# Sums of squares added on VectorE, the recurrent layer's heads token-major, and a small root that loads ScalarE's table early

## The chip, the cores and the metric

The kernel runs on one core of one Trainium2 chip. The metric is the device time of one launch in microseconds (us); the number given is the median of several launches. Everything is float32. TensorE does the matrix products, VectorE and ScalarE the elementwise work, and transfers are started from the queues of SyncE and GpSimd.

## The reference

The program is a chain of two transformer stacks over 256 tokens of width 1024. The first stack has two layers, each with a mixer (attention variants), a cross-attention to a memory and a gated feed-forward part. The second stack has four layers, each with a mixer (gMLP in layers 0 and 3, latent attention in layer 1, a gated recurrence in layer 2) and a convolutional feed-forward part. Every part starts with an RMS norm of the residual stream x, and the last norm makes the output:

```python
def rmsnorm(x, g):
    y = x * lax.rsqrt(jnp.mean(x * x, axis=-1, keepdims=True) + EPS)
    return y * g
```

The recurrent mixer ends so (o has 8 heads of 128 values per token; g is the last quarter of the projection h @ w_in):

```python
    o = rmsnorm(o, norm_g).reshape(B, S, nv) * jax.nn.silu(g)
    return o @ w_o
```

## The kernel before

x and h lie in SBUF as 8 tiles of 128 features by 256 tokens (features on the partitions). All weights come in one stream through a ring of 11 slabs of 8 tiles, which SyncE's queue refills as TensorE releases them. A linear of kind "F" makes one 128x256 output block after the other (8 blocks for the ones that end in x), with K matmuls each: K is 8 for `ab_out`, `nsa_out`, `mla_o`, `hg_o`, 4 for `memo0/1`, 16 for `gm_out0/3` and 22 for `down0/1` and `cdown0..3`. The blocks alternate between PSUM banks 0 and 1; VectorE (`residual`, L1054) adds block n into x[:, n], and ScalarE (`squares`, L801) then writes its square into h[:, n]. The order on every engine is written out by hand; engines meet at semaphores.

The norm: `with_norm` (L509) is called by `linear` after each block. `norm_part(k)` multiplies a 128x128 matrix of ones with the square tile h[:, k], so that the sum over features lands on all partitions of bank 4; it does so for k = n-2 after block n, and for k = 6 and 7 as well after the last block. Then ScalarE takes the root (L818), VectorE the reciprocal (L1042) and eight scaled products into h (L1045), in the second stack ScalarE adds a shift to each (L825), and TensorE's next linear takes each h tile as it comes. There are 16 norms: `mix0` and `mem` at the start have no linear ahead of them, the other 14 go through `with_norm`. After `mem0` and `mem1` TensorE first has `memk`, which reads the memory and not h.

In the down linears VectorE also reduces tiles of the modulation weights between the blocks (`ada_tile`, L1214; up to three per block), whose transfers GpSimd's queue starts.

The recurrent layer (layer 2; from L712 for TensorE, L988 for ScalarE, L1581 for VectorE): decayed scores are built in nine levels. For one level VectorE makes the arguments (L1624, L1625), ScalarE takes Exp (L1010), VectorE multiplies (L1637, L1639), TensorE multiplies (`level`) and VectorE places the result under masks (L1656). `level` runs between the blocks of `hg_v` and `hg_g`; ScalarE applies Silu to the gate blocks as they come (L1006), so that Exp and Silu alternate. After level 8, TensorE makes the 8 head outputs features-major (banks 7 and 3), VectorE copies them out (L1680), ScalarE squares (L1013), TensorE sums with ones, ScalarE takes 8 roots (L1016), VectorE takes for each head a reciprocal of 128x256 (L1684) and two products (L1685, L1687), and `hg_o` starts on head k as it is ready.

Of the kernel before, what the change touches and what calls it, by code (L numbers as in the profile page):

```python
# [8 lines left out]
ALU = mybir.AluOpType  # L9
# [139 lines left out]
def build(nc, stream, adaw_d, crow_d, xin, memin, cols_d, rows_d, gmrows_d, gmws_d, cmpw_d, consts_d, pos_d, out_d):  # L149
    with ExitStack() as ctx:  # L150
# [17 lines left out]
        stat = sb("stat", [P, 7, 56])  # L168
        att_s = sb("att_s", [P, 3, 3, 2])

        pair01 = ctx.enter_context(nc.psum_tensor("pair01", [P, 2, 512], F32))
# [74 lines left out]
        HGB = (5, 6, 7, 4)  # L246
        hg_lb = view(2048 * 8 + 3584, 8, DK)


# [120 lines left out]
        for i in range(LAYERS2):  # L370
            for n in ("mix", "ffn"):
                SHIFTED[f"{n}2_{i}"] = len(SHIFTED)

        SOURCE = {"mem0": "ab_out", "ffn0": "memo0", "mix1": "down0", "mem1": "nsa_out", "ffn1": "memo1",
# [64 lines left out]
        def _(pe):  # L439
# [173 lines left out]
            def body():  # L613
# [63 lines left out]
                for i in range(LAYERS2):  # L677
# [34 lines left out]
                    else:  # L712
# [24 lines left out]
                        n = hg_first[9]  # L737

                        pe.wait_ge(sem("hg_read"), n)
                        for hd in range(HG_HEADS):  # L740
                            if hd >= 2:
                                pe.wait_ge(sem("hg_o_read"), hd - 1)
                            ob = banks[TB[hd % 2]]
                            v = [hg_v[:, t, hd * P:hd * P + P] for t in range(TT)]
                            mm(ob[:, 0:P], v[0], hg_a[:, 0, hd, :], True, True)
                            mm(ob[:, P:TOK], v[0], hg_a[:, 2, hd, :], True, False)
                            mm(ob[:, P:TOK], v[1], hg_a[:, 1, hd, :], False, True).then_inc(sem("hg_o"), 1)
                        for hd in range(HG_HEADS):
                            pe.wait_ge(sem("hg_sq"), hd + 1)
                            if hd >= 2:  # L750
                                pe.wait_ge(sem("hg_sum_read"), hd - 1)
                            mm(banks[SB[hd % 2]][:, 0:TOK], ones, hg_e[:, hd, :], True, True).then_inc(sem("hg_sum"), 1)
                        linear("hg_o", lambda k: hg_q[:, k, :],
# [38 lines left out]
        def _(act):  # L792
# [122 lines left out]
            def body():  # L915
# [44 lines left out]
                for i in range(LAYERS2):  # L960
# [27 lines left out]
                    else:  # L988
# [12 lines left out]
                        lin = PLAN["hg_g"]  # L1001
                        for lv in range(8):
                            if lv >= 4:
                                for t in (2 * lv - 8, 2 * lv - 7):
                                    act.wait_ge(sem("mm_done"), lin.g0 + t + 1)
                                    nc.scalar.activation(hg_g[:, t, :], banks[(lin.g0 + t) % 2][:, 0:TOK],  # L1006
                                                         ACT.Silu).then_inc(sem("freed_act"), 1)
# [3 lines left out]
                        for hd in range(HG_HEADS):  # L1011
                            act.wait_ge(sem("hg_o_read"), hd + 1)
                            nc.scalar.activation(hg_e[:, hd, :], hg_b[:, hd, :], ACT.Square).then_inc(sem("hg_sq"), 1)  # L1013
                        for hd in range(HG_HEADS):
                            act.wait_ge(sem("hg_sum"), hd + 1)
                            nc.scalar.activation(hg_Q[:, hd, :], banks[SB[hd % 2]][:, 0:TOK], ACT.Sqrt, bias=EPS_COL,  # L1016
                                                 scale=1.0 / P).then_inc(sem("hg_sum_read"), 1)
                    squares(f"ffn2_{i}", x, h)
# [8 lines left out]
        def _(dve):  # L1027
# [25 lines left out]

            def residual(name, gate=None, between=None):  # L1054

                lin = PLAN[name]
                for n in range(DK):
                    g = lin.g0 + n
# [174 lines left out]
            def memory(i):  # L1233
# [30 lines left out]
                attention(*(U_MEM0, U_MEM1)[i])  # L1264
                residual(f"memo{i}")

            def body():
# [128 lines left out]
                attention(*U_DSA)  # L1396
                residual("ab_out")
                normalise("mem0", x, col("norm_mem0", 0, DK))
# [3 lines left out]
                up_tiles(0)  # L1402
                residual("down0", None, ada_tiles((2, 2, 2, 2, 2, 2, 1, 0)))
                V.engine_nop().then_inc(sem("hid_free"), 1)
# [84 lines left out]
                for kind in range(3):  # L1489
                    attention(*U_NSA[kind])  # L1490
                residual("nsa_out")
                normalise("mem1", x, col("norm_mem1", 0, DK))
# [10 lines left out]

                residual("down1", None, down1_between)
                for i in range(LAYERS2):
# [3 lines left out]
                    if i % 3 == 0:  # L1509
# [26 lines left out]
                        for f in range(GM_INNER // P):  # L1536
# [8 lines left out]
                            V.tensor_tensor(u, u, t2, ALU.mult).then_inc(sem("gm_mixed"), 1)  # L1545
                        residual(f"gm_out{i}", gate)
                    elif i % 3 == 1:
# [31 lines left out]
                        attention(*U_MLA)  # L1579
                        residual("mla_o", gate)  # L1580
                    else:  # L1581
# [95 lines left out]
                        placed(8)  # L1677
                        for hd in range(HG_HEADS):
                            dve.wait_ge(sem("hg_o"), hd + 1)
                            V.tensor_copy(hg_b[:, hd, :], banks[TB[hd % 2]][:, 0:TOK]).then_inc(sem("hg_o_read"), 1)  # L1680
                        for hd in range(HG_HEADS):
                            dve.wait_ge(sem("hg_sum_read"), hd + 1)
                            dve.wait_ge(sem("freed_act"), FREER[PLAN["hg_g"].g0 + hd][1])
                            link(V.reciprocal(hg_K[:, hd, :], hg_Q[:, hd, :]))  # L1684
                            link(V.scalar_tensor_tensor(hg_b[:, hd, :], hg_b[:, hd, :], col("hg_norm"), hg_K[:, hd, :],  # L1685
                                                        ALU.mult, ALU.mult))
                            V.tensor_tensor(hg_q[:, hd, :], hg_b[:, hd, :], hg_g[:, hd, :], ALU.mult  # L1687
                                            ).then_inc(sem("hg_y"), 1)
                        residual("hg_o", gate)
                    gate, gain = fin[:, 1, 0:DK], fin[:, 1, DK:2 * DK]  # L1690
# [11 lines left out]

                    residual(f"cdown{i}", gate, down_between)
                normalise("final", x, col("final", 0, DK), signal="out_ready")
# [131 lines left out]
```

## Time and profile before

| | us |
|---|---|
| median of 3 launches | 2768.84 (2767.59 to 2771.78) |
| the profiled execution's own time | 2776.93 |
| its span in the profile | 2775.1 |
| TensorE matmuls busy | 2612.3 (94% of the span) |
| VectorE busy | 1082.3 (39%) |
| ScalarE busy | 480.5 (17%) |
| TensorE's mean granted clock | 0.947 of 2.4 GHz |

The span is that of one profiled execution; the times are of launches without the profiler. One float32 matmul appears as two records of TensorE. Busy time of an engine overlaps with that of others; what sets the end is read in the chain of waits, which goes back from the last instruction to what released each step.

### The profile page before, as it was taken

What the parts mean: (1) busy time and instruction counts of PE and PEld (TensorE: products, weight loads), DVE (VectorE), ACT (ScalarE), POOL (GpSimd) and SP (SyncE); (2) the same over time, 40 slices, a digit from 0 to 9 for tenths busy, and PEclk for the clock granted to TensorE, in tenths of its full rate; (3) what the DMA queues carried; (4) which work ended last, traced back from release to release, by engine and by line L of the source; (5) the groups of instructions that cost most, each with busy time, mean ns of one, the idle gap of its engine ahead of it and who ended that gap; (6) DMA issues with size and microseconds to landing.
All of it is one profiled execution on the core that took longest, in us unless ns stands there. A gap on an engine that the chain in (4) does not pass through costs nothing.

```text
span 2775.1 us, 30582 instructions
## 1 busy us (share of the span) xinstructions
PE 2612.3 (94%) x11580; PEld 2052.4 (74%) x11580; DVE 1082.3 (39%) x2184; ACT 480.5 (17%) x1132; POOL 109.6 (4%) x211
## 2 busy tenths in 40 slices
PE   8789999998898999999999899999979999999997
PEld 4365888655567888588888478888768886688886
DVE  2744122245732022242563435633754552332321
ACT  1122100014402000111210222102322201102210
POOL 0000000000000000000011001110000010000000
PEclk9779999995699999999999999999989999999999
DMA  6123467530034566434778137783316774433441
GB/s 233 47 83 142 136 198 234 198 122 3 6 127 159 174 225 223 150 123 146 257 252 293 61 121 250 251 301 131 114 52 239 256 269 170 170 123 130 152 153 52
DMA packets 122174, 452.83 MB, mean 163 GB/s; under 512 B 13760, under 2 KB 13888, under 8 KB 121408
## 3 DMA queue, kind: packets, MB, share of 16 engines
q1 hardware_dynamic: 92880, 338.24, 35.2%
q0 software_dynamic: 29168, 112.80, 12.0%
q8 instruction: 93, 1.52, 0.2%
q14 instruction: 33, 0.27, 0.0%
HBM read 449.93 MB, written 1.05 MB: 163 GB/s over the span
## 4 chain that ended last, share of the span: by engine, by line
PE 88%; DVE 6%; issue 3%; ACT 2%; DMA 0%; SPq 0%; DVEq 0%; ACTq 0%; POOL 0%
PE pair L443 83%; PE bank L443 5%; DVE att_s L1136 1%; DVE arena L1131 1%; ACT arena L842 1%; PE bank L539 1%; DVE arena L1684 1%; ACT arena L854 0%; PE bank L566 0%; DVE arena L1545 0%; DVE arena L1541 0%; DMA cst<-consts_dram 0%; ACT arena L833 0%; DVE arena L1389 0%; DVE arena L1146 0%
## 5 line engine op out<-in xcount | busy, mean ns | idle before, releaser
L443 PE MATMUL pair<-h,ring 128*128 128x256 f32 x5120 | 1119.0, 382 | 26.3 <-issue 26.3
L443 PEld LDWEIGHTS pair<-h,ring 128*128 128x128 f32 x5120 | 979.9, 192 | 164.8 <-issue 29.8
L443 PE MATMUL pair<-arena,ring 128*128 128x256 f32 x3312 | 740.7, 383 | 12.6 <-DVE arena L1687 9.6
L443 PEld LDWEIGHTS pair<-arena,ring 128*128 128x128 f32 x3312 | 633.2, 192 | 106.5 <-DVE arena L1687 13.7
L443 PE MATMUL pair<-ring,h 128*128 128x512 f32 (+1 forms) x768 | 333.7, 596 | 20.9 <-issue 18.0
L443 PEld LDWEIGHTS pair<-ring,h 128*128 128x128 f32 x768 | 147.3, 196 | 202.9 <-issue 194.8
L1214 DVE CUSTOM_DVE_ANT_0 adat<-adat,crow,cols 128x1024 f32<-128x1024 f32 x192 | 241.8, 1277 | 4.2 <-DMA adat<-adaw_dram 4.2
L813 ACT ACTIVATE h<-x 128x256 f32<-128x256 f32 x120 | 49.2, 416 | 903.2 <-DVE x L1064 508.4
L1192 DVE SCALAR_TENSOR_TENSOR arena<-pair,cols,arena 128x255 f32<-128x255 f32 x176 | 84.9, 483 | 292.6 <-ACT arena L890 292.6
L890 ACT ACTIVATE arena<-pair,cols 128x256 f32<-128x256 f32 x176 | 99.2, 563 | 475.3 <-PE pair L443 475.3
L1064 DVE SCALAR_TENSOR_TENSOR x<-pair,fin,x 128x256 f32<-128x256 f32 x64 | 31.0, 484 | 378.2 <-PE pair L443 378.2
L443 PE MATMUL pair<-arena 128*128 128x128 f32 (+7 forms) x922 | 144.9, 368 | 20.6 <-DVE arena L1374 8.6
L401 POOL DMA_DIRECT2D adat<-adaw_dram x192 | 101.3, 528 | 1360.0 <-DVE mod L1214 1334.7
L443 PEld LDWEIGHTS pair<-arena 128*128 128x128 f32 (+4 forms) x922 | 99.2, 226 | 59.6 <-issue 20.6
L1077 DVE COPY arena<-pair 128x512 f32<-128x512 f32 (+1 forms) x58 | 39.1, 676 | 264.1 <-PE pair L443 264.1
L1180 DVE TENSOR_TENSOR arena<-pair,arena 128x256 f32<-128x256 f32 x44 | 18.7, 424 | 255.3 <-PE pair L443 255.3
L443 PE MATMUL bank<-arena 128*128 128x128 f32 (+2 forms) x640 | 89.1, 355 | 11.3 <-ACT arena L854 6.4
L1062 DVE TENSOR_TENSOR x<-pair,x 128x256 f32<-128x256 f32 x48 | 20.4, 424 | 201.7 <-PE pair L443 201.7
L443 PEld LDWEIGHTS bank<-arena 128*128 128x128 f32 (+2 forms) x640 | 62.8, 196 | 36.7 <-ACT arena L854 17.5
L1194 DVE SCALAR_TENSOR_TENSOR arena<-pair,cols,arena 128x254 f32<-128x254 f32 x176 | 84.7, 481 | 6.3
L842 ACT ACTIVATE arena<-arena,att_s 128x256 f32<-128x256 f32 (+2 forms) x160 | 67.6, 423 | 100.8 <-DVE att_s L1136 100.0
L443 PE MATMUL bank<-h,cst 128*128 128x256 f32 x240 | 71.1, 393 | 13.0 <-DMA cst<-consts_dram 10.8
(187 smaller groups left out, 1218.5 us busy)
## 6 DMA issues: line engine op xcount, KB each, us to landing
ring<-stream_dram SPq DMA_DIRECT2D x638, 512.0 KB, 3.9
adat<-adaw_dram POOLq DMA_DIRECT2D x192, 512.0 KB, 4.5
arena<-gmrows_dram POOLq DMA_DIRECT2D x2, 2560.0 KB, 10.1
arena<-cmpw_dram POOLq DMA_DIRECT2D x1, 2112.0 KB, 8.2
x<-x_in_dram SPq DMA_DIRECT2D x2, 512.0 KB, 4.6
arena<-mem_in_dram SPq DMA_DIRECT2D x1, 1024.0 KB, 12.5
arena<-gmws_dram POOLq DMA_DIRECT2D x2, 512.0 KB, 12.1
out_dram<-h POOLq DMA_DIRECT2D x1, 1024.0 KB, 4.1
```

The costliest lines, as they stand in the source:

```text
L401: pool.dma_start(adat[:, n % ADA_RING, :], adaw_d[n]).then_inc(sem(f"ada_in{n % ADA_RING}"), 16)
L443: return nc.tensor.matmul(out, lhsT, rhs, start=start, stop=stop)
L539: last = nc.tensor.transpose(banks[TB[j % 2]][:, b * P:b * P + P], src, ident)
L813: nc.scalar.activation(dst[:, k, :], src[:, k, :], ACT.Square).then_inc(sem("sq_done"), 1)
L842: ins = nc.scalar.activation(p, p, ACT.Exp, bias=att_s[:, u % 3, 0, e:e + 1], accum_out=att_s[:, u % 3, 1, e:e + 1])
L890: nc.scalar.activation(ybuf[:, t % 4, :], banks[g % 2][:, 0:TOK], ACT.Identity, bias=col(f"conv_b{i}", t), scale=col(f"conv_w{i}", 2 * 2 * ...
L1064: ins = V.scalar_tensor_tensor(x[:, n, :], b, gate[:, n:n + 1], x[:, n, :], ALU.mult, ALU.add)
L1077: V.tensor_copy(dst(n % 2, n // 2 * 512, w), banks[g % 2][:, 0:w]).then_inc(sem("freed_dve"), 1)
L1131: ins = V.scalar_tensor_tensor(p, s, un["scale"], un["mask"].unsqueeze(1).broadcast_to([P, 2, nk]), ALU.mult, ALU.add)
L1192: link(V.scalar_tensor_tensor(y[:, 1:TOK], b[:, 0:TOK - 1], col(f"conv_w{i}", 2 * FT + t), y[:, 1:TOK], ALU.mult, ALU.add))
L1194: V.scalar_tensor_tensor(y[:, 2:TOK], b[:, 0:TOK - 2], col(f"conv_w{i}", t), y[:, 2:TOK], ALU.mult, ALU.add).then_inc(sem("freed_dve"), 1)
L1214: V.tensor_tensor_reduce(out=w, in0=w, in1=crow[:, :], scale=1.0, scalar=col(f"ada_b{i}", t), op0=ALU.mult, op1=ALU.add, accum_out=mod[:, ...
```

## The change

Every `residual` also adds square tiles in place on VectorE: after block n it adds h[:, n-1] into h[:, 0]. TensorE then sums only h[:, 0] and h[:, 7], both after the last block. ScalarE takes a root of one column behind the sixth square. In the recurrent layer a gate block is only copied out and Silu is applied to four blocks at once; levels 3 to 6 follow gate blocks 0 to 3; the heads are made token-major ahead of gate blocks 4 to 7; their sums, roots and reciprocals are 128x8; the heads are turned back by TensorE's transposes. The diff, cut to its core:

```diff
+            def norm_sum(name):
+                pe.wait_ge(sem("sq_added"), SQ_ADDED[name])
+                mm(banks[SUMB][:, 0:TOK], ones, h[:, 0, :], True, False)
+                pe.wait_ge(sem("sq_done"), DK * (NORMS[name] + 1))
+                mm(banks[SUMB][:, 0:TOK], ones, h[:, DK - 1, :], False, True).then_inc(sem("sum_done"), 1)
-            def with_norm(norm, lag=2):
+            def with_norm(norm):
                 def after(n):
-                    if n >= lag:
-                        norm_part(norm, n - lag)
                     if n == DK - 1:
-                        for k in range(DK - lag, DK):
-                            norm_part(norm, k)
+                        norm_sum(norm)
...
# squares, ScalarE
                     nc.scalar.activation(dst[:, k, :], src[:, k, :], ACT.Square).then_inc(sem("sq_done"), 1)
+                    if lin is not None and k == DK - 3:
+                        nc.scalar.activation(spare[:, :], EPS_COL, ACT.Sqrt)
...
# residual, VectorE
+                def add_squares(k):
+                    dve.wait_ge(sem("sq_done"), DK * NORMS[norm] + k + 1)
+                    if k > 1:
+                        dve.wait_ge(sem("sq_added"), SQ_ADDED[norm] - (DK - 2) + k - 1)
+                    V.tensor_tensor(h[:, 0, :], h[:, 0, :], h[:, k, :], ALU.add).then_inc(sem("sq_added"), 1)
...
                     ins.then_inc(sem("freed_dve"), 1)
+                    if n >= 2:
+                        add_squares(n - 1)
                     if between is not None:
                         between(n)
...
# recurrent layer, TensorE (heads_out: per half, 4 matmuls for token tile 0 and 8 for tile 1, into banks 3, 2 / 5, 6;
# heads_turned: per half, two jobs of 4 transposes into banks 7 and 4, behind hg_scaled and hg_y)
-                        linear("hg_g", hin, None, lambda g: g % 2 == 1 and level(3 + g // 2))
-                        level(7)
-                        level(8)
+                        def after_gate(g):
+                            if g < 4:
+                                level(3 + g)
+                            if g == 3:
+                                level(7)
+                                level(8)
+                                pe.wait_ge(sem("hg_read"), hg_first[9])
+                                heads_out(0)
+                                heads_out(1)
+                            if g == 6:
+                                heads_turned(0)
+                            if g == 7:
+                                heads_turned(1)
+                        linear("hg_g", hin, None, after_gate)
...
# recurrent layer, ScalarE (gate_out: copy of a gate block; gates_silu: Silu of 128x1024)
                             if lv >= 4:
-                                for t in (2 * lv - 8, 2 * lv - 7):
-                                    ... Silu of gate block t
+                                gate_out(lv - 4)
...
+                        gates_silu(0)
+                        for q4 in range(2):
+                            for t in range(TT):
+                                act.wait_ge(sem("hg_o_read"), 2 * q4 + t + 1)
+                                nc.scalar.activation(hg_o2[:, t, 512 * q4:512 * q4 + 512],
+                                                     hg_o[:, t, 512 * q4:512 * q4 + 512], ACT.Square
+                                                     ).then_inc(sem("hg_sq"), 1)
+                            act.wait_ge(sem("hg_sums"), q4 + 1)
+                            r = stat[:, 1, 8 * q4:8 * q4 + 8]
+                            nc.scalar.activation(r, r, ACT.Sqrt, bias=EPS_COL, scale=1.0 / P).then_inc(sem("hg_root"), 1)
+                            gate_out(4 + 2 * q4)
+                            gate_out(5 + 2 * q4)
+                        gates_silu(4)
...
# recurrent layer, VectorE (heads_read: two copies of 128x512; heads_sums: two reductions of 128x512 to 4;
# heads_scale: reciprocal of 128x8, two products of 128x512; heads_gated: four products of 128x256 out of PSUM,
# turned head x norm gain x gate)
+                        heads_read(0)
+                        heads_sums(0)
+                        heads_read(1)
+                        heads_scale(0)
+                        heads_sums(1)
+                        heads_scale(1)
+                        heads_gated(0)
+                        heads_gated(1)
```

## Rows read from the trace of the kernel before

**Rows 1.** The page: the chain that ended last, shares by engine.
```profile
PE 88%; DVE 6%; issue 3%; ACT 2%; DMA 0%; SPq 0%; DVEq 0%; ACTq 0%; POOL 0%
```
**Rows 2.** Groups by form, whole span: count | busy us, mean ns | idle before, releasers.
```profile
L443 PE MATMUL bank<-h,cst 128*128 128x256 f32 x240 | 71.1, 393 | 13.0 <-DMA cst<-consts_dram 10.8 <-ACT h L813 1.7
L1010 ACT ACTIVATE arena<-arena 128x2048 f32<-128x2048 f32 x8 | 15.3, 1912 | 41.8 <-DVE arena L1625 41.7
L1064 DVE SCALAR_TENSOR_TENSOR x<-pair,fin,x 128x256 f32<-128x256 f32 x64 | 31.0, 484 | 378.2 <-PE pair L443 378.2
L818 ACT ACT_TABLE_LOAD x14 | 18.0, 1283 | 0.2
L1545 DVE TENSOR_TENSOR arena<-arena 128x256 f32<-128x256 f32 x32 | 13.6, 425 | 1.1
L870 ACT ACTIVATE stat<-stat 128x8 f32<-128x8 f32 x4 | 1.2, 301 | 35.5 <-DVE stat L1245 35.5
```
**Rows 3.** Chain in the last down linear: start us, us, what.
```profile
2708.11 0.43 PE bank L443 x2
2718.03 0.43 PE bank L443 x2
```
**Rows 4.** Timeline behind the last block of down1: start us, us, instruction.
```profile
1529.22 1.03 PE L443 MATMUL bank<-h,cst 128*128 128x256 f32 x4
1529.49 0.48 DVE L1064 SCALAR_TENSOR_TENSOR x<-pair,fin,x 128x256 f32<-128x256 f32 x1 [9.37 <-PE pair L443]
1530.01 0.42 ACT L813 ACTIVATE h<-x 128x256 f32<-128x256 f32 x1 [9.58 <-DVE x L1064]
1530.45 1.28 ACT L818 ACT_TABLE_LOAD   x1
1530.48 0.70 PE L443 MATMUL bank<-h,cst 128*128 128x256 f32 x2 [0.23 <-ACT h L813]
1535.16 3.75 PE L443 MATMUL pair<-ring,h 128*128 128x512 f32 x4 [3.98 <-issue]
```
**Rows 5.** Chain behind hg_o.
```profile
2095.24 3.46 issue
```
**Rows 6.** Chain behind ab_out.
```profile
210.14 27.47 PE pair L443 x64
237.60 0.87 PE bank L539 x8
```
**Rows 7.** Timeline of the start: the squares of the memory's norm, behind a root.
```profile
17.09 2.56 ACT L813 ACTIVATE arena<-arena 128x256 f32<-128x256 f32 x8 [0.52 <-DMA arena<-mem_in_dram]
```
**Rows 8.** Timeline of the recurrent layer.
```profile
1966.96 0.69 DVE L1665 COPY arena<-pair 128x512 f32<-128x512 f32 x1 [2.23 <-PE pair L443]
1980.78 7.07 PE L443 MATMUL pair<-h,ring 128*128 128x256 f32 x32
1987.68 1.95 PE L443 MATMUL bank<-arena 128*128 128x128 f32 x16
1991.26 7.07 PE L443 MATMUL pair<-h,ring 128*128 128x256 f32 x32
...
2012.48 1.23 DVE L1637 TENSOR_TENSOR arena<-arena 128x1024 f32<-128x1024 f32 x1 [3.41 <-ACT arena L1010]
2022.96 1.23 DVE L1637 TENSOR_TENSOR arena<-arena 128x1024 f32<-128x1024 f32 x1 [5.65 <-ACT arena L1010]
2026.10 2.02 PE L443 MATMUL bank<-arena 128*128 128x128 f32 x16 [3.24 <-DVE arena L1656]
2034.30 5.96 PE L443 MATMUL bank<-arena 128*128 128x128 f32 x48 [0.82 <-DVE arena L1656]
2064.27 9.82 PE L443 MATMUL pair<-arena,ring 128*128 128x256 f32 x34 [1.42 <-DVE arena L1687]
```
**Rows 9.** Windows on PE: us, PE busy (records), granted clock, DMA share, GB/s.
```profile
1108.00:1110.00 2.00, 1.42 (x2) 0.50 0.00 0
```
**Rows 10.** Timeline of PE behind the last block of gm_out0.
```profile
1297.40 6.87 PE L443 MATMUL pair<-h,ring 128*128 128x256 f32 x23 [3.98 <-issue]
```

More of the change, by code:

```diff
@@ L169, in build @@
         att_s = sb("att_s", [P, 3, 3, 2])
+        spare = sb("spare", [P, 1])
         pair01 = ctx.enter_context(nc.psum_tensor("pair01", [P, 2, 512], F32))
@@ L247, in build @@
         hg_lb = view(2048 * 8 + 3584, 8, DK)
+        hg_o, hg_o2 = view(2048 * 2, TT, 1024), view(2048 * 3, TT, 1024)
+        HG_OB, HG_TB = (3, 2, 5, 6), (7, 4)
         units = []
@@ L372, in build @@
                 SHIFTED[f"{n}2_{i}"] = len(SHIFTED)
+        SQ_ADDED = {}
+        for name in NORMS:
+            if name not in ("mix0", "mem"):
+                SQ_ADDED[name] = (DK - 2) * (len(SQ_ADDED) + 1)
         SOURCE = {"mem0": "ab_out", "ffn0": "memo0", "mix1": "down0", "mem1": "nsa_out", "ffn1": "memo1",
@@ L733, in body @@
                         linear("hg_v", hin, None, lambda g: g >= 1 and level(g - 1))
-                        linear("hg_g", hin, None, lambda g: g % 2 == 1 and level(3 + g // 2))
-                        level(7)
-                        level(8)
[L737 to L752, printed above, removed]
+                        def heads_out(q4):
+                            for t in range(TT):
+                                for e in range(4):
+                                    hd = 4 * q4 + e
+                                    out = banks[HG_OB[2 * q4 + t]][:, e * P:e * P + P]
+                                    v = [hg_v[:, b, hd * P:hd * P + P] for b in range(TT)]
+                                    if t == 0:
+                                        last = mm(out, hg_a[:, 0, hd, :], v[0], True, True)
+                                    else:
+                                        mm(out, hg_a[:, 2, hd, :], v[0], True, False)
+                                        last = mm(out, hg_a[:, 1, hd, :], v[1], False, True)
+                                last.then_inc(sem("hg_o"), 1)
@@ new lines, in heads_turned @@
+                        def heads_turned(q4):
+                            pe.wait_ge(sem("hg_scaled"), q4 + 1)
+                            for j in (2 * q4, 2 * q4 + 1):
+                                if j >= 2:
+                                    pe.wait_ge(sem("hg_y"), 2 * (j - 1))
+                                for b in range(4):
+                                    hd = 2 * j + b // 2
+                                    last = nc.tensor.transpose(banks[HG_TB[j % 2]][:, b * P:b * P + P],
+                                                               hg_o[:, b % 2, hd * P:hd * P + P], ident)
+                                last.then_inc(sem("hg_turned"), 1)
@@ L1010, in body @@
                             nc.scalar.activation(e[:, :, :], e[:, :, :], ACT.Exp).then_inc(sem("hg_exp"), 1)
[L1011 to L1017, printed above, removed]
+                        gates_silu(0)
+                        for q4 in range(2):
+                            for t in range(TT):
+                                act.wait_ge(sem("hg_o_read"), 2 * q4 + t + 1)
[8 more added lines that the diff above has]
+                        gates_silu(4)
                     squares(f"ffn2_{i}", x, h)
@@ L1052, in normalise, with residual @@
                     ins.then_inc(sem(signal), 1)
-            def residual(name, gate=None, between=None):
+            def residual(name, norm, gate=None, between=None):
                 lin = PLAN[name]
+                def add_squares(k):
[3 more added lines that the diff above has]
+                    V.tensor_tensor(h[:, 0, :], h[:, 0, :], h[:, k, :], ALU.add).then_inc(sem("sq_added"), 1)
                 for n in range(DK):
@@ L1264, in memory @@
                 attention(*(U_MEM0, U_MEM1)[i])
-                residual(f"memo{i}")
+                residual(f"memo{i}", f"ffn{i}")
             def body():
@@ L1396, in body @@
                 attention(*U_DSA)
-                residual("ab_out")
+                residual("ab_out", "mem0")
                 normalise("mem0", x, col("norm_mem0", 0, DK))
@@ L1402, in body @@
                 up_tiles(0)
-                residual("down0", None, ada_tiles((2, 2, 2, 2, 2, 2, 1, 0)))
+                residual("down0", "mix1", None, ada_tiles((2, 2, 2, 2, 2, 2, 1, 0)))
                 V.engine_nop().then_inc(sem("hid_free"), 1)
@@ L1490, in body @@
                     attention(*U_NSA[kind])
-                residual("nsa_out")
+                residual("nsa_out", "mem1")
                 normalise("mem1", x, col("norm_mem1", 0, DK))
@@ L1502, in down1_between @@
                         modulation(0, 0)
-                residual("down1", None, down1_between)
+                residual("down1", "mix2_0", None, down1_between)
                 for i in range(LAYERS2):
@@ L1545, in body @@
                             V.tensor_tensor(u, u, t2, ALU.mult).then_inc(sem("gm_mixed"), 1)
-                        residual(f"gm_out{i}", gate)
+                        residual(f"gm_out{i}", f"ffn2_{i}", gate)
                     elif i % 3 == 1:
@@ L1579, in body @@
                         attention(*U_MLA)
-                        residual("mla_o", gate)
+                        residual("mla_o", f"ffn2_{i}", gate)
                     else:
@@ L1677, in body @@
                         placed(8)
[L1678 to L1688, printed above, removed]
@@ L1689, in body, with heads_read, heads_sums @@
-                        residual("hg_o", gate)
+                        def heads_read(q4):
+                            for t in range(TT):
+                                dve.wait_ge(sem("hg_o"), 2 * q4 + t + 1)
+                                V.tensor_copy(hg_o[:, t, 512 * q4:512 * q4 + 512], banks[HG_OB[2 * q4 + t]][:, :]
+                                              ).then_inc(sem("hg_o_read"), 1)
+                        def heads_sums(q4):
+                            for t in range(TT):
+                                dve.wait_ge(sem("hg_sq"), 2 * q4 + t + 1)
+                                ins = V.tensor_reduce(stat[:, 1, 8 * q4 + 4 * t:8 * q4 + 4 * t + 4],
+                                                      hg_o2[:, t, 512 * q4:512 * q4 + 512].rearrange(
+                                                          "p (h d) -> p h d", d=P), AX_X, ALU.add)
+                            ins.then_inc(sem("hg_sums"), 1)
@@ new lines, in heads_scale @@
+                        def heads_scale(q4):
+                            dve.wait_ge(sem("hg_root"), q4 + 1)
+                            r = stat[:, 1, 8 * q4:8 * q4 + 8]
+                            link(V.reciprocal(r, r))
+                            for t in range(TT):
+                                v = hg_o[:, t, 512 * q4:512 * q4 + 512].rearrange("p (h d) -> p h d", d=P)
+                                ins = V.tensor_tensor(v, v, r[:, 4 * t:4 * t + 4].unsqueeze(2).broadcast_to([P, 4, P]),
+                                                      ALU.mult)
+                            ins.then_inc(sem("hg_scaled"), 1)
@@ new lines, in heads_gated @@
+                        def heads_gated(q4):
+                            dve.wait_ge(sem("hg_silu"), q4 + 1)
+                            for j in (2 * q4, 2 * q4 + 1):
+                                dve.wait_ge(sem("hg_turned"), j + 1)
+                                for e in range(2):
+                                    hd = 2 * j + e
+                                    V.scalar_tensor_tensor(hg_q[:, hd, :], banks[HG_TB[j % 2]][:, e * TOK:e * TOK + TOK],
+                                                           col("hg_norm"), hg_g[:, hd, :], ALU.mult, ALU.mult
+                                                           ).then_inc(sem("hg_y"), 1)
@@ L1690, in body @@
+                        heads_read(0)
[6 more added lines that the diff above has]
+                        heads_gated(1)
+                        residual("hg_o", f"ffn2_{i}", gate)
                     gate, gain = fin[:, 1, 0:DK], fin[:, 1, DK:2 * DK]
@@ L1701, in down_between @@
                                 modulation(i + 1, 0)
-                    residual(f"cdown{i}", gate, down_between)
+                    residual(f"cdown{i}", f"mix2_{i + 1}" if i + 1 < LAYERS2 else "final", gate, down_between)
                 normalise("final", x, col("final", 0, DK), signal="out_ready")
```

11 lines of the change are left out of this document (8 added, 3 removed).

## The prediction
> **What bounds the kernel now.** I read the page first. In the chain that ended last TensorE holds 88% and VectorE 6% [rows 1]: time is won where TensorE has less to do, or where the chain leaves it. So I took the groups by form, then the chain in a down linear, then the timeline behind a last block and through the recurrent layer, and last the granted clock.
>
> Inside a linear TensorE is never late: behind the last down linear's blocks two records of the ones product, 0.43 us, recur 9.92 us apart [rows 3], and the rest of the 9.92 is the block's own 22 products. One such product per square tile gives 15 x 8 x 2 = 240 records [rows 2]; `mem`'s norm has another operand. VectorE idled 378.2 us before the 64 gated residual products, waiting for TensorE [rows 2]: it is far ahead.
>
> Behind a last block the chain goes [rows 4]: VectorE's product (1529.49, 0.48), ScalarE's square (1530.01, 0.42), then two things side by side: a table load from 1530.45 to 1531.73, and the last ones product from 1530.48 to 1531.18. The root waits for the load. TensorE starts again at 1535.16, 3.98 us after its product. Behind `hg_o`, where a root ran just before and no load is needed, it is 3.46 [rows 5]: the load costs 0.52 there. Between 1529.22 and 1530.25 TensorE does the products of the sixth and seventh square for nothing, since it would wait anyway.
>
> **The sums of squares.** 14 norms change. Of each one's eight products those for k = 0 to 4 stand between blocks and go: 14 x 5 x 0.43 = 30.1 us, all on the path. Those for k = 5 and 6 stood in the wait: nothing. Bounds: nothing else stands in for them inside the linear, so 28 to 31.
>
> VectorE gets 6 x 14 adds, 0.43 each [rows 2]. They lie beside the linears: a block lasts 9.5 us in the down linears, against 0.48 + 0.43 + three tile reductions; in `memo`, K = 4, it lasts 1.73 (four products of 0.43), against 0.43 + 0.43. The add behind block n waits for the square of block n-1, written a block earlier; what is queued behind it (modulation tiles, the next residual) has a whole block of slack, as two PSUM banks alternate. So nothing; were the cover gone, 84 x 0.43 = 36 us.
>
> **The tail of a norm.** At the end VectorE adds the seventh square after its last residual: about 1529.97 to 1530.40, while ScalarE squares the last tile until 1530.43. TensorE can start at 1530.48 with h[:, 0] and then needs h[:, 7]: 0.43 + 0.70, to 1531.61. The table is there already, so the root starts at 1531.64 in place of 1531.73: 0.1 us gained. If the first product fits in ahead of the last square it is 0.5 gained; if both take 0.70, 0.2 lost. Eleven tails are of this kind (`ffn0`, `mix1`, `ffn1`, `mix2_0..3`, `ffn2_0, 1, 3`, `final`): -1.1, bounds -6 to +2. Behind `hg_o` no load was waited for, so the second product is 0.4 lost; behind `ab_out` and `nsa_out` TensorE goes on with `memk` at once [rows 6], so nothing but that product counts, 0.4 each: +1.3. Together +0.2. The small root is cheap cover for the load: it stands ahead of the seventh square, at 1.28 + 0.30 (128x8 [rows 2], taken for 128x1) + 0.42 = 2.0 us of ScalarE; only in `memo` is a block shorter, and there the seventh square is 0.3 late and the eighth is not.
>
> On the load the row shows 1283 ns, and the square before and the root behind join it without a gap. The Trainium skill ("ScalarE: Activation LUTs", What ACT_TABLE_LOAD costs) counts a drain of some 1380 ns to every switch. By that rule each of the eleven tails would save 1.4 us more, 15 us in all, and the forecast would be 2703. Rows 4 speak against it: load and square lie 0.02 us apart, and the 3.98 leaves no room for it. I leave it out.
>
> **The recurrent layer.** A pair of gate blocks takes 6.90 and a level 3.58 on TensorE (1980.78, 1987.68, 1991.26 [rows 8]), a period of 10.48, in which VectorE waits 3.41 for ScalarE: its own work is 7.07 a level. The change puts one gate block beside a level: 3.45 + 3.58 = 7.03 on TensorE, 7.07 on VectorE, about even. Placing it step by step, with gate block 0 at 1980.78:
> - levels 3, 4, 5, 6 start at 1984.2, 1991.3, 1998.3, 2005.3; gate block 3 ends at 2005.3. No Silu, hence no load, stands between the Exps.
> - copy of block 3 (0.4), Exp 1.91, so level 7's products on VectorE at 2007.7. Before, they began at 2022.96 and level 7 on TensorE at 2026.10, the heads at 2034.30: the whole chain is 15.3 us earlier, heads at 2019.0.
> - heads: the same 24 products, 5.96 before, to 2024.7. Gate blocks 4 and 5 to 2031.6; copies free their banks. Meanwhile the first half is copied, squared, summed, rooted and scaled: seven VectorE operations of 0.69 (the 128x512 copy in rows 8), done by 2027.
> - ScalarE takes the second half's squares only behind the copy of gate block 5: 2032.0 to 2033.3; sums and products on VectorE to 2035.9. Gate block 6 to 2035.1, first turn (8 transposes, 0.87 at full clock [rows 6], 1.1 with waits) to 2036.3, gate block 7 to 2039.8, second turn to 2041.
> - `hg_o` takes heads 0 to 3 to 2042.7. Heads 4 to 7 need the second Silu: copy of block 7 to 2040.2, load 1.28, Silu of 128x1024 about 1.06 (between 0.42 for 256 columns and 1.91 for 2048), to 2042.6, then four products of 0.48: head 7 starts at 2044.6.
>
> Before, head 7 started at 2064.27: 19.7 us gained. There TensorE ran at 1.2 GHz, after long idling: the 34 records from 2064.27 took 9.82 [rows 8], against 34 x 0.216 = 7.34 at 2.4 GHz (6.90 / 32 in the gate blocks). TensorE is nearly full now, so 2.5 more: 22.2. Bounds: 17 (level 7's 2 us of waiting lets the clock fall, VectorE sets the pace in each level) and 24 (the last waits are hidden). The skill's page "TensorE: Matmul & The Clock Gate", Part 4, says that transposes do not count as activity. Only 2.2 us of them stand here, between full gate blocks; by that rule the clock could fall near 2041 and cost some 2 us, which is within the bound.
>
> **The clock behind the tails.** After most tails TensorE's granted clock is down to its lower level (0.50 at 1108 [rows 9]). What that costs: 17 records of 128x512 took 9.75 (not in these groups at the full level; one is two of 0.216), and 23 of 128x256 1.90 more than 23 x 0.216 [rows 10]. I take 1.7 to 3.4 per tail. Afterwards the last wait is shorter (3.4 for 3.98) but the one before the sum grows from 0.23 to 1.05, since nothing fills it. So the fall can come sooner. I add 2 us; bounds -6 to +12.
>
> **Sum.** -30.1 + 0.2 - 22.2 + 2 = -50.1 us. On the profiled execution's own 2776.9 that is 2726.8; the median of launches is 8.1 lower, and the same sum gives 2768.8 - 50.1 = 2718.7. I say 2718.5.
>
> **Rivals.**
> - The clock takes more: every one of the nine or so slowed tails goes from the shorter to the longer low stretch, and the recurrent layer gets its lower bound. +1.7 x 9 - 2 + 5 = +18, 2737. For it: 1.05 us without work ahead of the sum. Against: the wait behind it is half a us shorter. Chance 0.12.
> - The clock takes less: a shorter last wait leaves four or five more tails at 2.4 GHz, and the first sum product fits in ahead of the last square: -10 - 5, 2704. Chance 0.08.
> - The sums gave TensorE nothing: if block time were set by the weight stream, the 30.1 would turn into waits for slabs, and only the recurrent layer's gain and the tails would stay: 2749. Against: no wait of TensorE for the ring shows, the 9.92 is all products. Chance 0.03.
> - Slower than before: the sparser tail keeps the clock down far into the next linear. TensorE then loses half of each further us. From 50 us over the eleven following stages on, 4.6 us each, so a low stretch 9 us longer than now, it is slower; at 12 it gives 2785. The rows of before have low stretches of only a few us, with full work ending them. Chance 0.02.
> - The change does not do what it says: if squares behind the small root needed a table of their own, the load would be back in the tail. The memory's squares ran straight behind a root, eight in 2.56 us with no load [rows 7], so squares live with the root. Even then the tail is only as before plus 0.4: 2724. Chance 0.02.
>
> **How the numbers follow.** Forecast 0.73 (2718.5, its own range 2711 to 2727). Range 2706 to 2735: it takes in most of the first two rivals. Within 0.2% (5.5 us, about what a measurement of this kernel tells from no change) would need the slow rival halfway, 0.02 with what is left over; slower 0.02; faster 0.96.
>
> **What would show it.** Down blocks follow each other at 9.50, the ones products on h are 14 x 2 x 2 + 16 = 72 records in place of 240; the table load lies ahead of the seventh square and the root follows the sum by 0.03; first product of the next linear 5.6 us behind the last block; heads at 38 us behind gate block 0; `hg_o`'s eighth product 64 us behind it, in place of 83.5. Wrong would be: blocks still 9.9 apart, VectorE's add late at the tail, or granted clock below 1 beyond some 7 us behind a tail.

## The result and the profile after

The changed kernel takes 2721.57 us (median of 4 launches, 2716.96 to 2722.06) against 2770.31 of the kernel before on the same chip (4 launches): 48.7 us less, ratio 0.982, 95% interval 0.9803 to 0.9837. The forecast was 50.1 less, 2718.5. The profiled execution took 2721.67, its span is 2719.9.

The page of the changed kernel, the chain's shares by engine [rows 1]:

```profile
PE 89%; DVE 6%; issue 3%; ACT 2%; DMA 0%; SPq 0%; DVEq 0%; POOL 0%; ACTq 0%
```

The groups of the changed kernel by form, in the columns of [rows 2]:

```profile
L1116 DVE TENSOR_TENSOR h<-h 128x256 f32<-128x256 f32 x84 | 34.9, 415 | 0.0
L451 PE MATMUL bank<-h,cst 128*128 128x256 f32 x72 | 22.2, 445 | 23.6 <-DVE h L1116 12.6 <-DMA cst<-consts_dram 10.9
L850 ACT ACT_TABLE_LOAD x14 | 18.0, 1283 | 0.2
L850 ACT ACTIVATE spare<-stat 128x1 f32<-128x1 f32 x14 | 2.8, 203 | 0.2
```

The 240 records of ones products are 72, and 84 adds stand on VectorE; L850's 14 roots of one column are the small root, and each brings one table load. The chain through the second stack's first up and down linears is one piece, with no product between blocks, where before a ones product stood behind each block of the down linear from the third on [rows 3]:

```profile
1277.02 230.99 PE pair L451 x1056
```

The timeline behind the last block of down1 [rows 4]:

```profile
1508.10 0.48 DVE L1125 SCALAR_TENSOR_TENSOR x<-pair,fin,x 128x256 f32<-128x256 f32 x1 [8.60 <-PE pair L451]
1508.50 0.42 DVE L1116 TENSOR_TENSOR h<-h 128x256 f32<-128x256 f32 x1
1508.62 0.42 ACT L848 ACTIVATE h<-x 128x256 f32<-128x256 f32 x1 [9.15 <-DVE x L1125]
1508.97 1.13 PE L451 MATMUL bank<-h,cst 128*128 128x256 f32 x4 [0.98 <-DVE h L1116]
1510.14 0.47 ACT L855 ACTIVATE rstd<-bank,stat 128x256 f32<-128x256 f32 x1 [1.11 <-PE bank L451]
1513.56 2.05 PE L451 MATMUL pair<-ring,h 128*128 128x512 f32 x2 [3.46 <-issue]
```

From the start of the last residual to the next linear it was 1535.16 - 1529.49 = 5.67, now it is 5.46. There is no load behind the last square any more; the two products take its place.

The recurrent layer of the changed kernel [rows 8]:

```profile
1980.80 1.91 ACT L1057 ACTIVATE arena<-arena 128x2048 f32<-128x2048 f32 x1
1985.89 2.02 PE L451 MATMUL bank<-arena 128*128 128x128 f32 x16 [1.82 <-DVE arena L1719]
1994.09 2.94 PE L451 MATMUL bank<-arena 128*128 128x128 f32 x24 [0.81 <-DVE arena L1719]
1996.87 2.84 PE L451 MATMUL pair<-arena 128*128 128x128 f32 x24
2006.93 1.15 ACT L1062 ACTIVATE arena<-arena 128x512 f32<-128x512 f32 x2
2014.83 1.28 ACT L1049 ACT_TABLE_LOAD   x1
2016.12 1.06 ACT L1049 ACTIVATE arena<-arena 128x1024 f32<-128x1024 f32 x1
2017.75 4.58 PE L451 MATMUL pair<-arena,ring 128*128 128x256 f32 x20 [0.75 <-DVE arena L1775]
```

The first gate block starts at 1955.97 here (behind level 2, in the chain), at 1980.78 before. The heads come 38.1 us behind it (53.5 before), head 4's product 61.8, head 7's about 63.1 (three products of 0.43 later; 83.5 before).

Cut at the first product of the next linear behind each norm, the changed profile is 1.9 to 2.4 us shorter in five of the stages, between 0.1 longer and 3.0 shorter in six others, 24.2 shorter in the recurrent layer, and 12.4 in the stage with the sparse attention of the first stack (256.0 against 268.4), where the change takes out 2.2. The other 10 go with the clock; window rows of the attention's part, before first, then changed:

```profile
584.00:770.00 186.00, 161.15 (x1035) 102.24 (x1034) 102.52 (x342) 71.51 (x265) 1.07 (x2) 0.67 0.09 30
```
```profile
580.00:755.00 175.00, 145.90 (x1029) 92.57 (x1028) 101.81 (x341) 71.51 (x264) 1.07 (x2) 0.75 0.09 31
```

The columns are TensorE's matmuls, its weight loads, VectorE, ScalarE and GpSimd busy, then the granted clock. The code there is the same, the granted clock is 0.67 before and 0.75 after. So the two spans differ by 55.2 and the medians only by 48.7: the profiled execution of before, 2776.93, is 6.6 above the median of its launches. Where unprofiled launches lose time is not recorded.

### The profile page after: what moved, and what is told of

The parts are those of the page before. It is cut to its first block, busy times and chain, and to the rows that moved or that the text cites. A ratio compares the mean times of both kernels' runs of the same rounds, so it can differ in the third digit from the quotient of the medians.

```text
span 2719.9 us, 30380 instructions
## 1 busy us (share of the span) xinstructions
PE 2560.4 (94%) x11412; PEld 2014.1 (74%) x11412; DVE 1097.5 (40%) x2258; ACT 474.3 (17%) x1133; POOL 109.6 (4%) x211
## 4 chain that ended last, share of the span: by engine, by line
PE 89%; DVE 6%; issue 3%; ACT 2%; DMA 0%; SPq 0%; DVEq 0%; POOL 0%; ACTq 0%
PE pair L451 85%; PE bank L451 4%; DVE att_s L1199 1%; DVE arena L1194 1%; ACT arena L879 1%; PE bank L551 1%; ACT arena L891 0%; DVE arena L1608 0%; DVE arena L1604 0%; PE bank L578 0%; DMA cst<-consts_dram 0%; ACT arena L870 0%; DVE arena L1452 0%; DVE arena L1209 0%; DVE h L1116 0%
## 5 line engine op out<-in xcount | busy, mean ns | idle before, releaser
L451 PEld LDWEIGHTS pair<-h,ring 128*128 128x128 f32 x5120 | 984.8, 193 | 163.4 <-issue 26.7
L451 PE MATMUL pair<-arena,ring 128*128 128x256 f32 x3312 | 722.5, 380 | 3.7 <-issue 2.1
L451 PE MATMUL bank<-arena 128*64 128x128 f32 (+2 forms) x616 | 81.8, 340 | 11.4 <-ACT arena L891 8.2
L451 PEld LDWEIGHTS bank<-arena 128*64 128x64 f32 (+2 forms) x616 | 57.6, 188 | 35.2 <-ACT arena L891 18.3
L578 PE MATMUL bank<-cst,arena 128*128 128x128 f32 x200 | 46.0, 354 | 30.0 <-DVE arena L1209 17.8
```

The source lines that it names most:

```text
L451: return nc.tensor.matmul(out, lhsT, rhs, start=start, stop=stop)
L578: ins = nc.tensor.transpose(tb[:, (2 * e + kt) * P:(2 * e + kt + 1) * P], pb[:, u % 3, e, kt * P:kt * P + P], ident)
```

## The experiments

Their baselines, the kernel before on the same chip, were 2771.94, 2772.24 and 2772.47 us in the three batches. The changed kernel's 2721.57 stands beside a baseline of 2770.31, 1.6 to 2.2 lower; a comparison with it across batches is uncertain by at least as much.

**Squares summed on VectorE, alone.** The recurrent layer is that of before and there is no small root; the rest is the change's `norm_sum` and `add_squares`. Of the change these two lines are left out:

```diff
-                    if lin is not None and k == DK - 3:
-                        nc.scalar.activation(spare[:, :], EPS_COL, ACT.Sqrt)
```

> The kernel before with the squares summed on VectorE and nothing else (no small root, recurrent layer as before). Theory (each part pays for itself, on TensorE's path): 70 products of 0.43 us go, -30.1; the tail stays as before, since the table load (1.28) ends 0.17 later than the two products (1.13) after the last square; +0.4 behind ab_out, nsa_out and hg_o; the clock takes up to 6 us more. So -23 to -29 us against before. Rival (the inline products cost nothing, block time is set elsewhere): within 3 us of before. Rival (VectorE's adds delay the frees of the banks): gaps between blocks of the down linears above 9.50 us.

Measured: 2742.65, 29.3 less than before (ratio 0.9886, 0.986 to 0.9912). The inline products were on the path. The first rival falls by the time, the second by the profile: the blocks of the last down linear follow each other 9.50 us apart, where from the third on they were 9.93 apart before.

**The small root, alone.** The kernel before with these two lines added:

```diff
+                    if lin is not None and k == DK - 3:
+                        nc.scalar.activation(spare[:, :], EPS_COL, ACT.Sqrt)
```

> The kernel before with the small root behind the sixth square and nothing else. Theory: with only one product behind the last square, the root starts 0.03 us behind it instead of behind the load, so 11 tails fall from 3.98 to 3.46 us (3.44 to 2.92 without a shift): -5.7 us, the clock giving or taking 3. Rival (a drain of 1.4 us goes with every switch of tables): -5.7 - 15 = -21 us. Rival (squares behind the small root need a load of their own): a second load in each tail, 0 or above.

Measured: 2765.43, 6.5 less (0.9976, 0.9963 to 0.9989). Its chain behind the last block of down1, start, us, what:

```profile
1520.51 0.50 DVE x L1067
1521.03 0.42 ACT h L814
1521.50 0.70 PE bank L444 x2
1522.20 3.46 issue
```

3.46 in place of 3.98: the load of 1.28 was worth 0.52 in a tail, 5.7 in eleven tails. Neither the 21 us of the first rival nor a second load of the other one shows.

**The recurrent layer, alone.** The changed kernel with the old norms (the calls of `add_squares` and the small root are out too):

```diff
+                    if n >= lag:
+                        norm_part(norm, n - lag)
                     if n == DK - 1:
-                        norm_sum(norm)
+                        for k in range(DK - lag, DK):
+                            norm_part(norm, k)
```

> The kernel before with the new recurrent layer and nothing else. Theory: hg_o's eighth product comes 19.7 us earlier and the slow clock behind it goes, -22 us against before (bounds -17 and -24). Rival (most of it is the clock, not the shorter order): the granted clock during hg_o full but the product less than 10 us earlier. Together the three single parts would give -30 + 1 - 5.7 - 22 = about -57 against the measured -49 if they simply added up; the theory says they overlap in the tail (root and second product compete, 4 us) and in the clock.

Measured: 2752.54 (2745.87 to 2755.88), 19.4 less (0.9928, 0.9902 to 0.9954), an interval that holds 22. In its profile the recurrent layer's stage is 21.9 shorter than before (189.9 against 211.8). The tail behind `hg_o` is 0.5 longer in it, 5.67 for 5.15: the last table before it is now that of Silu, so the root there needs a load again. The three single gains add to 55.2, the whole is 48.7. Of the 6.5 between them 3.2 is the small root, which gives 5.7 alone and 2.5 beside the second product (next run); the rest is no more than the medians scatter.

**The changed kernel without the small root.**

> The changed kernel without the small root. Theory: in the changed kernel the second ones product stands behind the last square too and takes most of the time that the load took, so the load hidden is worth only 0.17 to 0.2 us in 11 tails: this kernel is 1 to 3 us slower than the changed one (2722 to 2725). Rival (the root is worth what it is alone): 6 us slower, 2727. Rival (drain): 17 us slower, 2738.

Measured: 2718.74 (2713.71 to 2720.14), so by time not slower than 2721.57, though the theory and both rivals had it slower; the two are of different batches and their spreads overlap. In the trace the root's worth is plain, the timeline behind down1 (columns as in [rows 4]):

```profile
1506.51 1.13 PE L451 MATMUL bank<-h,cst 128*128 128x256 f32 x4 [0.98 <-DVE h L1114]
1506.59 1.28 ACT L853 ACT_TABLE_LOAD   x1
1507.88 0.47 ACT L853 ACTIVATE rstd<-bank,stat 128x256 f32<-128x256 f32 x1
1511.30 2.05 PE L451 MATMUL pair<-ring,h 128*128 128x512 f32 x2 [3.67 <-issue]
```

The load ends 0.2 us behind the products: 3.67 against 3.46. It is so in twelve tails and not in eleven, since `hg_o`'s root needs a load too once Silu stands ahead of it: 0.21 x 12 = 2.5 us. The launches don't resolve it.

**Squares 6 and 7 left to TensorE, which has time for the first of them.**

```diff
                 mm(banks[SUMB][:, 0:TOK], ones, h[:, 0, :], True, False)
+                pe.wait_ge(sem("sq_done"), DK * (NORMS[name] + 1) - 1)
+                mm(banks[SUMB][:, 0:TOK], ones, h[:, DK - 2, :], False, False)
...
-                    if n >= 2:
+                    if 2 <= n < DK - 1:
                         add_squares(n - 1)
```

> The changed kernel, but VectorE adds only the squares 1 to 5, and TensorE sums h[:, 0], h[:, 6] and h[:, 7], the first two in the wait for the last residual and square. Theory: one product (0.70) stands behind the last square instead of two (1.13): 0.43 us less in each of 14 tails, -6.0 us, the gap ahead of the sum is filled for 0.86, and the clock gives or takes 5: 2711 to 2720, middle 2715.5. Rival (the clock's fall hangs on the gap ahead of the sum): low stretches of 6.8 us shrink or go in several tails, 6 us more gained. Rival (the third product costs its 0.43 on the path): no change, 2721.

Measured: 2716.51, but from 2704.33 to 2725.11: unclear by itself. In its profile one product of 0.70 stands behind the last square, as expected, but a tail is shorter by 0.32 (5.14 from the last residual to the next linear, 5.46 before that) and not by 0.43, since the first of the two products starts 0.11 earlier than the single one does here: 14 x 0.32 = 4.5 us in place of 6.0. The stage with the sparse attention ran at clock 0.65 and took 265.7, 10 us longer than in the profile of the changed kernel.

**TensorE kept at work in the wait behind the sum.** The kernel `e6_warm` adds to the changed one (`e7_warm3` has 3 and 3 products):

```diff
+                if name not in ("mem0", "mem1", "final"):
+                    for _ in range(7 if name in SHIFTED else 6):
+                        mm(banks[7][:, 0:TOK], ones, cst[:, 0:TOK], True, True)
```

> The changed kernel with 7 more 128x256 products on constants behind each sum (6 where no shift follows), in 11 tails, into a bank that nobody reads; they fill 2.6 to 3.0 of the 2.9 to 3.5 us in which TensorE waits for the next h. Theory (the half clock behind each tail comes from that wait): the granted clock stays at 2.4 GHz behind the tails, and the 27.8 us that the profile of the changed kernel loses there (low stretch behind the resume, halved) come back: -22 to -28 us, 2694 to 2700. Rival (the extra products run into the arrival of h): the next linear starts up to 0.3 us late, +3 us. Rival (the clock falls whatever TensorE does in the wait): 2722.

> As the kernel with filled tails, but with only 3 more products (1.3 us), so that 1.6 to 2.2 us without work are left. Theory (what counts is how long TensorE is without work): some of the tails keep the full clock, some fall later; between 2700 and 2718. Rival (any gap brings the fall): 2722. Rival (any work in the wait is enough): as with all of them, 2695 to 2700.

Measured: 2695.79 (2693.22 to 2695.92) with all, 2697.77 with three. Repeated in the next batch:

> The changed kernel with filled tails once more, as the partner of the other three on the same chip: 2694 to 2697 by both theories.

It gave 2694.38. Twelve microseconds behind the end of gm_out0, window rows (columns as above) of before, changed, all and three products; with three, this is one of the five tails that lost nothing:

```profile
1293.00:1305.00 12.00, 8.02 (x30) 6.50 (x30) 6.57 (x12) 5.30 (x11) 0.00 (x0) 0.86 0.17 54
```
```profile
1273.00:1285.00 12.00, 8.54 (x27) 6.75 (x26) 5.81 (x11) 4.34 (x10) 0.00 (x0) 0.72 0.13 45
```
```profile
1266.00:1278.00 12.00, 11.56 (x54) 9.83 (x54) 7.17 (x13) 4.82 (x11) 0.53 (x1) 1.00 0.26 87
```
```profile
1261.00:1273.00 12.00, 9.84 (x46) 8.33 (x45) 7.44 (x14) 5.19 (x12) 0.53 (x1) 1.00 0.26 87
```

And TensorE's timeline of the same place, with all the products:

```profile
1265.75 1.13 PE L451 MATMUL bank<-h,cst 128*128 128x256 f32 x4 [0.91 <-DVE h L1119]
1266.72 3.18 PE L451 MATMUL bank<-cst 128*128 128x256 f32 x14
1270.34 8.01 PE L451 MATMUL pair<-h,ring 128*128 128x256 f32 x36 [0.44 <-issue]
```

The next linear comes as soon as h allows, and 36 records take 8.0 us, 0.22 each; in the changed kernel, 24 take 8.23. In the profile with all the products none of the eleven tails loses anything to the clock; with three, six still lose about 1.7 us each, 10.2 in all. By time the kernel with three products lies in the range of the rival that any work in the wait is enough; its profile speaks for the theory. There the wait left without work is 1.62 us in three tails, and none of them loses; it is 2.16 in the other eight, and six of them lose. So not every gap brings the fall, and a shorter one brings it less often; with the same 2.16 us it came or stayed out.

**The same filling in the kernel before.**

> The kernel before with 7 more products on constants (6 where no shift follows) behind each sum in 11 tails, nothing else changed. Theory (the half clock behind the tails comes from the wait alone): the 21.7 us that the profile of before loses there come back: -20 to -22, 2749 to 2752. Rival (the gain of the filled tails hangs on the changed kernel's wider gap ahead of the sum): less than 15 us.

Measured: 2747.85, 24.6 less (0.9907, 0.988 to 0.9934), slightly more than expected, and the interval holds the 20 to 22. In its profile none of the eleven tails loses anything to the clock. The wider gap ahead of the sum is not needed for the gain.

**Filled, and without the small root; filled, and with early summing.**

> The changed kernel with filled tails, without the small root. With the clock held, the spread is small, so the root's own worth can be seen. Theory: 11 tails x 0.17 = 1.9 us slower than the filled kernel with the root, and the gap behind the sum 3.08 and 3.62 us in place of 2.92 and 3.46. Rival (the root is worth nothing or costs, as the median of the pair without filled tails has it): 0 or up to 3 us faster.

> Filled tails and early summing of squares 1 to 5, without the small Silu. Theory: 0.43 x 14 = 6.0 us below the filled kernel, and 0.8 above the kernel that has the small Silu too (2688.6): about 2689.5. Rival (early summing gains nothing once the clock is held): 2695.

Measured: 2696.46 (2694.09 to 2701.49) and 2692.04 (2690.12 to 2695.4), against 2694.38 (2692.78 to 2698.03) in the same batch. Without the root it is 2.1 slower, as the theory has it, but the spreads overlap. Early summing gives 2.3 where 6.0 were expected. With the clock held its worth can be read stage by stage: ten of the stages that end in a changed tail are 0.31 to 0.32 shorter than in the profile of its partner, so some 4.5 us in 14 tails were to be had, not 6.0. The stage with the sparse attention is 3.5 longer, at clock 0.65 again. By time, both stay unclear.

**All together**, with one more line in the recurrent layer:

```diff
                             nc.scalar.activation(r, r, ACT.Sqrt, bias=EPS_COL, scale=1.0 / P).then_inc(sem("hg_root"), 1)
+                            if q4 == 1:
+                                nc.scalar.activation(spare[:, :], EPS_COL, ACT.Silu)
```

> Early summing (squares 1 to 5 on VectorE), filled tails (7 and 6 products) and, in the recurrent layer, a Silu of one column behind the second root, so that the second Silu's table is loaded before the last gate block. Theory: -6 (tails) -26 (clock) -0.8 (wait for head 4) against the changed kernel: 2687 to 2692. Rival (early summing and filling overlap, both act by the clock): 2694 to 2700. It would beat both kernels.

Measured: 2688.61 (2688.03 to 2690.08), ratio to before 0.9697 (0.9678 to 0.9715). It beats both kernels, the changed one by 33 us. The single worth of the small Silu, 0.8 by the forecast, is less than the launches resolve. In the chain its `hg_o` follows the second turn without a stop:

```profile
1991.22 0.87 PE bank L773 x8
1992.10 7.99 PE pair L451 x37
```

## Why the prediction was right, step by step

- **Inline products, -30.1.** Held: alone, with its tail costs, the sum on VectorE gave 29.3.
- **VectorE's adds, nothing.** Held: 84 adds of 0.42, none of which delays a block; the six pairs of an up and a down linear run through in one piece each, of 230.5 to 231.0 us. Only the seventh add releases TensorE, at the place forecast and 0.1 us earlier.
- **Tail, -0.1 each.** It is -0.21 in eleven tails, since VectorE's add starts 0.08 ahead of the end of the residual's record. That is 1 us in all. The root is worth 5.7 alone (6.5 measured) and 2.5 beside the second product: the two edits compete for the same microsecond.
- **The drain of a table switch.** The small root alone gave 6.5 us, and without it the root follows its load by 0.01 us. The Trainium skill ("ScalarE: Activation LUTs", What ACT_TABLE_LOAD costs) adds a drain of some 1380 ns to every switch to another set; by that figure, as an estimate, it would have given 21 us. The measurement decides against the rule here.
- **Recurrent layer, -22.2.** Levels, copies, squares and turns lie where the forecast put them: heads 38.1 us behind gate block 0 (38.2 forecast), head 7 at 63.1 (63.8 forecast), Silu of 128x1024 at 1.06. The slow start of `hg_o` is gone: 120 records in 26.18 us, 0.218 each, where the first 34 took 9.82 before. TensorE's clock was at full level through the layer, transposes included (window row below, from level 5 to the first products of `hg_o`). The Trainium skill ("TensorE: Matmul & The Clock Gate", Part 4) says that the full clock doesn't engage for transposes; the two groups of 0.87 us between full linears did not lower it here. Alone the layer measured 19.4 with an interval that holds 22, and its stage is 21.9 shorter.
- **Clock behind the tails, +2.** This was the term furthest off in the profiles. Half the time between the next linear's start and the clock's rise, over the eleven tails that a linear follows (`hg_o`'s among them), is 21.7 us in the profile of before and 27.8 in that of the changed kernel: +6.1. Before, one tail kept the full clock and four lost only 1.6 to 1.7; afterwards each lost 2.1 to 2.9. Behind gm_out0, 23 records took 6.87 before (4.97 at full clock, 1.9 lost [rows 10]) and 24 took 8.23 after (5.18, 3.0 lost; second row below). The forecast's reason, the gap of 0.9 us ahead of the sum, is not shown. For it: the other kernels with that gap lost 28.3 (sums alone) and 27.0 (without the root), those with the old summing 21.9 (recurrent layer alone) and 15.3 (small root alone). Against it: early summing fills the gap and still lost 24.8. Its profile and that of the small root alone have the same TensorE records, to 0.01 us, in the 6.4 us ahead of the next linear in all eleven tails (rows below), and lost 24.8 and 15.3. So a single profile's loss can scatter by more than the 6.1 that was to be explained, and whether the two kernels differ by as much stays open.
- **The sum.** Inline products -30.1, eleven tails -2.3, three other tails +0.9 (behind hg_o 5.46 for 5.15), recurrent layer -22.4 (its stage's 24.2, less 2.15 of inline products, and with the 0.3 put back that its longer tail took), clock +6.1: -47.8 by what the traces showed, against 48.7 measured and 50.1 forecast. The remaining difference between the profiles, 55.2 in all, is the sparse attention's clock (-10.2) and 2.7 at the start. That the forecast came within 1.4 us of the gain owes something to luck: the launches of either kernel spread over 5 to 6 us, the tails' 1 us more and the clock's 4 us more pull against each other, and the median of before itself moved by 1.5 (2768.84, then 2770.31).

The clock in the recurrent layer of the changed kernel (window row: us, PE busy, granted clock, DMA share, GB/s), and TensorE's timeline behind gm_out0:

```profile
1977.00:2018.00 41.00, 37.62 (x250) 1.00 0.21 72
```
```profile
1277.02 8.23 PE L451 MATMUL pair<-h,ring 128*128 128x256 f32 x24 [3.46 <-issue]
```

TensorE behind the last block of down1, with the small root alone and with early summing; from the first row's start to the next linear it is 5.42 us in both:

```profile
1520.24 1.03 PE L444 MATMUL bank<-h,cst 128*128 128x256 f32 x4
1521.50 0.70 PE L444 MATMUL bank<-h,cst 128*128 128x256 f32 x2 [0.23 <-ACT h L814]
```
```profile
1513.93 1.03 PE L451 MATMUL bank<-h,cst 128*128 128x256 f32 x4
1515.19 0.70 PE L451 MATMUL bank<-h,cst 128*128 128x256 f32 x2 [0.23 <-ACT h L850]
```

## What to carry to other kernels

Price an instruction on the bounding engine by where it stands: five of eight products were on the path, two were free, and one was part of the tail. Two edits that shorten the same tail don't add up, so draw the tail with both in it. And where a kernel has regular waits of some 3 us on TensorE, look at the granted clock behind them before polishing the wait itself: keeping TensorE at work there gave 26 us, some ten times the 2.5 that the small root is worth in the changed kernel.

## What was not expected

- The clock's cost behind eleven waits of 2.9 to 4.0 us, 22 to 28 us, comes back almost whole when the wait is filled with products that nobody uses: 24.6 in the kernel before, 25.8 in the changed one. Three products of the seven, which fill 1.3 us, already give 23.8. But its profile, 22.5 shorter, has 16.2 of that behind the tails, and 6.5 in the sparse attention and at the start, which the edit doesn't touch; with all seven the stages behind the tails are 26.7 shorter.
- Part of the spread lies where no edit touched anything: in the sparse attention, at clock 0.65 to 0.77 in the six profiles in which it was read and 252 to 268 us for the stage in all of them, and in the start, 37.2 to 41.2 us to the first product behind the memory's norm. It hides effects of 2 us, like the small root's in the changed kernel.
